# Attention scores from stacked query parts in a two-layer hybrid decoder trunk

## The reference, cut to what matters

```
q  = rope(q)                    # (512, 8, 64), key head kv serves query heads 4*kv + j, j = 0..3
ks, kw = rope(k_sel), rope(k_win)            # (512, 2, 64) each
for br, k, v in ((0, ks, vs), (1, kw, vw)):
    s = einsum('qd,kd->qk', q[:, 4*kv + j], k[:, kv]) * 64 ** -0.5
    p = softmax(where(key <= query, s, -1e30))
    o[br] = p @ v[:, kv]
out = g0 * o_cmp + g1 * o[0] + g2 * o[1]
x = layer_norm(x * alpha + mix(out, scan, pool) @ w_out)
```

## Time and profile before

| | us |
|---|---|
| median of 3 runs | 1748.84 (1747.89 to 1749.04) |
| the profiled execution | 1748.62 |
| its span on the core | 1746.5 |
| TensorE matmuls busy | 1723.6 (99% of the span) |
| VectorE busy | 945.5 (54%) |
| ScalarE busy | 648.7 (37%) |
| GpSimd busy | 115.8 (7%) |
| granted TensorE clock, mean | 0.999 of full speed |

### The profile page before, as it was taken

The page is one execution under the profiler, slowest core; times in us unless marked ns, Lnnn a source line. Parts: engine busy times, 40 slices in busy tenths (PEclk is TensorE's granted clock), DMA queues, the critical chain, the costliest instruction groups (busy, mean ns, idle before and its releaser), DMA issues.

```text
span 1746.5 us, 26759 instructions
## 1 busy us (share of the span) xinstructions
PE 1723.6 (99%) x10172; PEld 1404.4 (80%) x10172; DVE 945.5 (54%) x1527; ACT 648.7 (37%) x1151; POOL 115.8 (7%) x241
## 2 busy tenths in 40 slices
PE   7999999999999999999999999999999999999998
PEld 6788777788888888888888877777888888888886
DVE  5888777554364444422359877864453644444224
ACT  4334666422242222221343346654222422222113
POOL 5600000000000000000045000000000000000000
PEclk9999999999999999999999999999999999999999
DMA  8443111122422222222374431112233222222222
GB/s 270 151 119 89 55 50 48 61 97 99 168 85 84 96 96 97 96 96 97 109 234 122 106 90 56 43 50 72 93 116 118 85 96 96 96 96 96 97 97 85
DMA packets 67134, 174.88 MB, mean 100 GB/s; under 512 B 14448, under 2 KB 25744, under 8 KB 66784
## 3 DMA queue, kind: packets, MB, share of 16 engines
q1 hardware_dynamic: 42560, 151.01, 25.1%
q10 hardware_dynamic: 21888, 13.64, 3.3%
q0 software_dynamic: 2592, 8.92, 1.7%
HBM read 162.27 MB, written 7.08 MB: 97 GB/s over the span
## 4 chain that ended last, share of the span: by engine, by line
PE 91%; DVE 4%; DVEq 2%; ACT 1%; DMA 1%; issue 1%; SPq 0%; ACTq 0%
PE ps L541 20%; PE ps L543 20%; PE ps L542 20%; PE ps L583 5%; PE ps L584 5%; PE ps L582 5%; PE ps L899 2%; PE ps L886 2%; PE ps L872 2%; PE ps L715 1%; PE ps L573 1%; PE ps L562 1%; DMA raw<-wstream 1%; PE ps L564 1%; PE ps L563 1%
## 5 line engine op out<-in xcount | busy, mean ns | idle before, releaser
L541 PE MATMUL ps<-xh,whi 128*128 128x512 f32 x1312 | 519.6, 396 | 2.5 <-ACT gates L1277 2.5
L543 PE MATMUL ps<-xh,wlo 128*128 128x512 f32 x1312 | 511.4, 390 | 0.0
L542 PE MATMUL ps<-xl,whi 128*128 128x512 f32 x1312 | 510.9, 389 | 0.0
L1465 DVE TENSOR_TENSOR wlo<-raw,whi 128x1024 fp32r<-128x1024 f32 x254 | 312.0, 1229 | 324.0 <-ACT whi L1019 318.0
L1019 ACT ACTIVATE whi<-raw 128x1024 fp32r<-128x1024 f32 x248 | 262.0, 1056 | 331.7 <-PE ps L584 216.7
L541 PEld LDWEIGHTS ps<-xh,whi 128*128 128x128 f32 x1312 | 246.4, 188 | 53.0 <-issue 3.6
L543 PEld LDWEIGHTS ps<-xh,wlo 128*128 128x128 f32 x1312 | 246.2, 188 | 52.5
L542 PEld LDWEIGHTS ps<-xl,whi 128*128 128x128 f32 x1312 | 246.6, 188 | 49.0 <-issue 0.5
L582 PE MATMUL ps<-whi,hh 128*128 128x512 f32 x336 | 131.3, 391 | 0.0
L584 PE MATMUL ps<-whi,hl 128*128 128x512 f32 x336 | 130.8, 389 | 0.0
L583 PE MATMUL ps<-wlo,hh 128*128 128x512 f32 x336 | 130.7, 389 | 0.0
(11 more groups left out here) (367 smaller groups left out, 2380.1 us busy)
## 6 DMA issues: line engine op xcount, KB each, us to landing
raw<-wstream SPq DMA_DIRECT2D x264, 512.0 KB, 3.2
w<-w1s SPq DMA_DIRECT2D x16, 512.0 KB, 7.2
sm<-smalls POOLq DMA_DIRECT2D x2, 1060.0 KB, 7.0
xt<-xin ACTq DMA_DIRECT2D x4, 512.0 KB, 6.4
scratch_u<-pa ACTq DMA_DIRECT2D x8, 256.0 KB
toep<-scratch_k ACTq DMA_DIRECT2D x4, 512.0 KB
toep_b<-scratch_k ACTq DMA_DIRECT2D x4, 512.0 KB
xt<-xin POOLq DMA_DIRECT2D x4, 512.0 KB, 4.2
```

Source lines behind the costliest of these rows:

```text
L541: pe.matmul(ps[:, bank, :], wh, hi[:, k, :], start=first and i == 0, stop=False)
L542: pe.matmul(ps[:, bank, :], wh, lo[:, k, :], start=False, stop=False)
L543: m = pe.matmul(ps[:, bank, :], wl, hi[:, k, :], start=False, stop=last and i == len(blocks) - 1)
L1465: dve.tensor_tensor(wlo[:, c % 2, :], raw[:, c % 2, :], whi[:, c % 2, :].bitcast(f32), SUB).then_inc(lo_ready, 1)
```

## The change

It has four parts.

1. `scores` makes four matmuls over all 128 rows, two for each key head. Its stationary operand for key head v (`q_parts[j][v]`) has the high part of that head's queries on one half of the partitions and their low part on the other; its moving operands are `k_high[v]` and `k_low[v]`, the head's keys on both halves. So high by high and low by high come out of one product, and high by low together with low by low, which was left out before, out of the other. The mask is added as before.
2. For this GpSimd copies keys to the other half by three DMAs of 256 KB (`kro_b`, and `kro` itself), after waits on the rotated keys, on the compressed keys and on the first output matrices of the scan. `key_parts` makes two casts and two subtractions of 128 x 1024 in place of one each, and signals `keys_split`. `query_parts` becomes `query_high` (one addition as before, and two casts of 64 x 512) and `query_low` (two subtractions of 64 x 512 with output on the other half). In the loop `query_low` is at u = 5, `gelu_low` goes from u = 5 to 6. Buffers are moved for it; `prob` has two slots in place of three.
3. In the loop, `pool_means` goes from j = 2, u = 4 to 7 to j = 2, u = 6 and 7, and j = 3, u = 3 and 4. ScalarE does the gate output of the first slab of j = 3 ahead of the wait on `gelu_arg`.
4. At the layer norms `turn_back` of the first half comes after three of the six products of the first remaining slab; ScalarE and VectorE do the four groups of the first half ahead of the split of the second slab of the next stage; `first_pair` waits for the first slab, and for the second only ahead of its own quarters.

```diff
     at = big_at + 12288
-    prob = more("prob", [P, 3, 2, S])
+    prob = more("prob", [P, 2, 2, S])
     probt = more("probt", [P, 2, 2, S])
+    kh_b = place("kh_b", at, [P, 2, S], f32r)
+    at += 2 * S
...
+    q_parts = ((q_a0, q_b0), (q_a1, q_b1[0]), (q_a0, q_b0), (q_a1, q_b1[1]))
+    kh_a = place("kh_a", used["sm"][0] + SM["bre"][0], [P, 2, S], f32r)
+    kl_a = place("kl_a", used["kro"][0], [P, 2, S], f32r)
+    kl_b = place("kl_b", used["sm"][0] + SM["wg"][0], [P, 2, S], f32r)
+    kro_b = place("kro_b", used["kl_b"][0], [P, 2, S])
+    k_high, k_low = (kh_a, kh_b), (kl_a, kl_b)
...
                 pool.memset(r8m[:, :, 0:1], 0.0).then_inc(eph_ready, 1)
+                wait(krot_done, l * 3 + 3)
+                pool.wait_ge(kc_psum, l + 1)
+                pool.wait_ge(mats_ready[0], l * 2 + 1)
+                for rows in (slice(0, HD), slice(HD, P)):
+                    pool.dma_start(kro_b[rows, :, :], kro[HD:P, :, :]).then_inc(keys_moved, 16)
+                wait(keys_moved, l * 48 + 32)
+                pool.dma_start(kro[HD:P, :, :], kro[0:HD, :, :]).then_inc(keys_moved, 16)
...
-                token_products(ends[0][0], ends[0][1], 1, 3, k, hi, lo, False).then_inc(slab_done, 1)
+                token_products(ends[0][0], ends[0][1], 1, 3, k, hi, lo, False, (0,))
                 turn_back(n, 0, rt)
+                token_products(ends[0][0], ends[0][1], 1, 3, k, hi, lo, False, (1,)).then_inc(slab_done, 1)
...
-                pe.wait_ge(lo_ready, at + 4)
+                pe.wait_ge(lo_ready, at + 3)
                 for g in range(4):
                     x_quarter(at, 0, g, n * 8)
+                pe.wait_ge(lo_ready, at + 4)
...
-                    qh, ql = qhis[i // 8], qlos[i // 8]
-                    for a, b in ((qh, krh), (ql, krh), (qh, krl)):
-                        for kv in range(2):
-                            rows = slice(64 * kv, 64 * kv + 64)
-                            pe.matmul(ps[:, sbank(i) + kv, 0:n], a[rows, P * t:P * t + P], b[rows, br, 0:n],
-                                      start=a is qh and b is krh, stop=False)
+                    for kv in range(2):
+                        q = q_parts[i // 8][kv]
+                        for k in (k_high[kv], k_low[kv]):
+                            pe.matmul(ps[:, sbank(i) + kv, 0:n], q[:, P * t:P * t + P], k[:, br, 0:n], start=k is k_high[kv], stop=False)
...
                 pe.wait_ge(masks_ready, 2)
+                pe.wait_ge(keys_split, l + 1)
                 pe.wait_ge(q_ready, l * 4 + 2)
...
-                split_end_hi(next_slab + 1, 2, next_slab - 4)
                 for g in range(4):
                     gained(n, 0, g, rt, last)
+                split_end_hi(next_slab + 1, 2, next_slab - 4)
                 split_next_hi(next_slab + 2, next_slab - 2)
...
                         if j < 3:
                             query_out(j + 1, n, 6)
+                        else:
+                            gate_out(13, n, 6)
                         act.wait_ge(gelu_arg, l * 5 + j + 2)
...
-                    if j == 3 and u in (1, 3, 5):
+                    if j == 3 and u in (3, 5):
                         gate_out(13 + u // 2, n, 6)
...
-                split_end_lo(next_slab + 1, 2)
                 second_stats(n, 2, next_slab + 2)
-                for g in range(3):
+                for g in range(4):
                     halves(n, 0, g, rt, last)
                 second_stats(n, 3, next_slab + 2)
                 variances(1)
-                halves(n, 0, 3, rt, last)
+                split_end_lo(next_slab + 1, 2)
                 scalars(n, 1)
...
                     dve.drain()
-                    dve.tensor_copy(krh[:, :, :], kro[:, :, :])
-                    dve.drain()
-                    tt(krl[:, :, :], kro[:, :, :], krh[:, :, :].bitcast(f32), SUB)
+                    dve.wait_ge(keys_moved, l * 48 + 48)
+                    whole = (kro, kro_b)
+                    for v in range(2):
+                        dve.tensor_copy(k_high[v][:, :, :], whole[v][:, :, :])
+                    dve.drain()
+                    for v in range(2):
+                        x = tt(k_low[v][:, :, :], whole[v][:, :, :], k_high[v][:, :, :].bitcast(f32), SUB)
+                    x.then_inc(keys_split, 1)
...
-                def query_parts(j):
+                def query_high(j):
                     q, q_shift, _ = att_bufs(j)
                     dve.drain()
                     tt(q[:, :], qt1[:, :], q_shift[:, :], ADD)
                     dve.drain()
-                    dve.tensor_copy(qhis[j][:, :], q[:, :])
-                    dve.drain()
-                    tt(qlos[j][:, :], q[:, :], qhis[j][:, :].bitcast(f32), SUB).then_inc(q_ready, 1)
+                    for v in range(2):
+                        rows = slice(HD * v, HD * v + HD)
+                        dve.tensor_copy(q_parts[j][v][rows, :], q[rows, :])
+
+                def query_low(j):
+                    q = att_bufs(j)[0]
+                    dve.drain()
+                    for v in range(2):
+                        rows, other = slice(HD * v, HD * v + HD), slice(HD - HD * v, P - HD * v)
+                        x = tt(q_parts[j][v][other, :], q[rows, :], q_parts[j][v][rows, :].bitcast(f32), SUB)
+                    x.then_inc(q_ready, 1)
...
                 rope(0)
-                query_parts(0)
+                query_high(0)
+                query_low(0)
                 scan(l * 4 + 3, 3)
...
+                    if u == 5 and j < 3:
+                        query_low(j + 1)
                     if k0 == 0 and at < 3:
                         split_lo(hl_, first_slab(j) + at + 1)
...
                     if u == 4 and j < 3:
-                        query_parts(j + 1)
-                    if u == 5:
+                        query_high(j + 1)
+                    if u == 6:
                         gelu_low(j)
...
-                    if j == 2 and u > 3:
-                        x = pool_means(u - 4)
-                        if u == 7:
+                    if j == 2 and u > 5:
+                        pool_means(u - 6)
+                    if j == 3 and u in (3, 4):
+                        x = pool_means(u - 1)
+                        if u == 4:
                             x.then_inc(pool_ready, 1)
```

More of the change, by code:

```diff
@@ L141, in build_program @@
     toep = own("toep", [P, 8, P])
-    sm = own("sm", [P, NSM])
     nrm = own("nrm", [P, L, 32])
@@ L151, in build_program @@
     dmaskb = own("dmaskb", [P, P], mybir.dt.bfloat16)
+    sm = own("sm", [P, NSM])
     pa = place("pa", big_at + 8192, [P, 10, S])
@@ L169, in build_program @@
     st = more("st", [P, 16, GP])
+    at = big_at + 17408
     u8_c = more("u8_c", [P, 8, NCH])
@@ L227, in build_program @@
     qraws = (qraw_a, qraw_b)
[L228 to L234, removed]
+    q_a0 = place("q_a0", big_at + 19200, [P, S], f32r)
+    q_b0 = place("q_b0", big_at + 19712, [P, S], f32r)
+    q_a1 = place("q_a1", used["nsh"][0] + 3 * S, [P, S], f32r)
+    q_b1 = [place("q_b1_%d" % n, used["nsl"][0] + n * S, [P, S], f32r) for n in (2, 3)]
+    q_parts = ((q_a0, q_b0), (q_a1, q_b1[0]), (q_a0, q_b0), (q_a1, q_b1[1]))
[4 more added lines that the diff above has]
+    k_high, k_low = (kh_a, kh_b), (kl_a, kl_b)
     qt1 = place("qt1", used["toep"][0] + S, [P, S])
@@ L574, in residual, with token_products @@
                                   start=m == 0, stop=False, is_transpose=True)
-            def token_products(high, low, fh, t, k0, hi, lo, last):
+            def token_products(high, low, fh, t, k0, hi, lo, last, parts=(0, 1)):
                 dst = ps[:, tile_bank(fh, t), :]
-                for q in range(2):
+                for q in parts:
                     a, b = hi[:, k0 + q, P * t:P * t + P], lo[:, k0 + q, P * t:P * t + P]
@@ L885, in turned @@
                             bank, at = turned_at(i, kv)
-                            m = pe.transpose(ps[:, bank, at + P * k:at + P * k + P], prob[:, i % 3, kv, P * k:P * k + P], ident)
+                            m = pe.transpose(ps[:, bank, at + P * k:at + P * k + P], prob[:, i % 2, kv, P * k:P * k + P], ident)
                     m.then_inc(s_tpsum, 1)
@@ L1341, in exps @@
                     for kv in range(2):
-                        x = act.activation(prob[:, i % 3, kv, 0:n], ps[:, sbank(i) + kv, 0:n], ACT.Exp,
+                        x = act.activation(prob[:, i % 2, kv, 0:n], ps[:, sbank(i) + kv, 0:n], ACT.Exp,
                                            bias=tiny[:, 28 + 8 * (i % 3) + kv:29 + 8 * (i % 3) + kv],
@@ L1349, in scale @@
                     act.wait_ge(s_ratio, l * 32 + (i + 1))
-                    act.activation(prob[:, i % 3, 0, 0:n], prob[:, i % 3, 0, 0:n], ACT.Copy, scale=tiny[:, 52 + 2 * (i % 3):53 + 2 * (i % 3)])\
+                    act.activation(prob[:, i % 2, 0, 0:n], prob[:, i % 2, 0, 0:n], ACT.Copy, scale=tiny[:, 52 + 2 * (i % 3):53 + 2 * (i % 3)])\
                        .then_inc(p_first, 1)
@@ L1930, in scale @@
```

(2 more changed lines are left out.)

5 lines of the change are left out of this document (3 added, 2 removed).

## The result

| | before | changed |
|---|---|---|
| median | 1748.93 (1747.89 to 1750.36, 7 runs) | 1755.56 (1754.89 to 1757.49, 7 runs) |
| the profiled execution | 1748.62 | 1757.19 |
| its span | 1746.5 | 1755.0 |
| granted clock, mean | 0.999 | 0.994 |

The ratio is 1.0039 [1.0029, 1.0049]: the changed kernel is 6.6 us slower. Forecast were 1742.0 and a range of 1737.5 to 1747.5, with 0.09 for slower. The prediction was wrong, in direction too.

What follows compares the result with a forecast made beforehand. It took TensorE, with matmuls running 99% of the span, as the bound. Terms of -6.8 + 3.8 - 1.1 - 2.5 + 0 = -6.6 us against the profiled 1748.62 gave 1742.0, range 1737.5 to 1747.5.

Steps and rivals of the forecast that it cites:

- Keys on GpSimd: Three key DMAs before the attention: GpSimd idles from 75.7 us, they are needed by 150.87, so they cost nothing.
- the other terms: All but the key copies: scores -6.8, prologue +3.8, loop -1.1, gate output -2.5, layer norms 0; sum -6.6 us.
- The two on the slower side: Scores: the entrance gap stays, 1752.3 us, chance 0.08; both gaps stay and side-by-side pairs count, 1758.4 us, chance 0.05.
- the larger gain: Rival at layer norms and scores: norms win their 2.1 us and scores 0.15 each, 1737.7 us; chance 0.12.
- the gain at 128 keys: Scores of 128 keys, last transpose to mask: 0.68 us before, 0.57 after, gain given as 0.12.
- Scores: Attention scores on TensorE: four full products replace three half-array pairs, mean gain 0.11 us over 60 scores, -6.8 us.
- Both gaps: Scores, entering and leaving the three half-array pairs: extra time of about 0.19 + 0.09 us, saved by full products.
- Prologue: Attention's start: added VectorE casts and subtractions for keys and queries delay TensorE 1.9 us a layer, +3.8 us.
- Loop: Attention loop: VectorE work moved between units removes TensorE's wait for copied probabilities, -1.1 us.
- Gate output and norms: Gate output ahead of the tanh's wait removes TensorE waits, -2.5 us; at layer norms the wait only moves, 0.

Runs made afterwards that it cites:

- before_with_copies: Kernel before plus only the waits and three key copies, at the changed kernel's place, into a buffer nobody reads: 1763.71 us, 1.0082.
- keys_after_toep: Changed kernel with GpSimd's first key copies waiting until the scan's first matrix, `toep`, has landed: 1746.66 us, 0.9983 of the kernel before.
- no_copies: Changed kernel without the three key copies, both key heads' operands made from `kro` as it stands: 1744.13 us, 0.9972 of the kernel before.
- keys_after_toep_b: Changed kernel with GpSimd's key copies waiting until the scan's next matrix, `toep_in[1]`, has landed: 1746.06 us, 0.9983 of the kernel before.
- gate_and_norms_only: Kernel before with only the gate output moved ahead of the tanh and the change's fourth part, the layer norms: 1746.57 us, 0.9982.
- no_copies_pairs: Changed kernel without the key copies and with scores again as three pairs of half-array products: 1751.49 us, 1.0011 of the kernel before.
- the new order of the prologue: `keys_after_toep_b` with both maxima ahead of the compressed scores and score 0 scaled before the slab split: 1739.67 us, 0.9946 of the kernel before.
- third_copy_late: Changed kernel with the first two key copies at their place, only the third behind the landing of `toep`: 1753.70 us, 1.0023.

## Why the prediction was wrong

**The step that failed** is "Keys on GpSimd": "Cost nothing; if the copies came 60 us late they would go straight onto the chain above". It asked one question of the three DMAs, whether they would be through before `key_parts` needs them, and they were: the last was issued at 99.99 us with a due time near 150. It did not ask what else the 16 DMA engines were doing at 92 us. The last of the copies' waits to end, for the compressed keys (L845, [16.40 <-PE ps L845] in the timeline), let them go at 92.60 us, just as ScalarE starts the scan's round trip, and that had no room: its products came directly at the end of the work ahead of them. `before_with_copies` shows the cost without the rest of the change, `keys_after_toep` shows the rest without the cost. By medians:

| | us |
|---|---|
| forecast | 1742.0 |
| the other terms, short by (`no_copies`, 1744.13) | +2.1 |
| copies, even late (`keys_after_toep_b`, 1746.06) | +1.9 |
| copies at the place of the change (1755.56) | +9.5 |

Against the kernel before, timed beside it (1749.10), `no_copies` gains 5.0 us of the 6.6 forecast, so the second row is 1.6 us by that count. The third row is within the noise, as said above.

The last row is not the waits alone. In the profiled executions the changed kernel reaches the query's products of layer 1 7.65 us later than `keys_after_toep_b` (161.78 and 154.13). TensorE stands for 6.03 us, and the work behind, up to the next slab, takes 6.40 us in place of 4.56, so 1.84 us more at the lower clock (less 0.23 us by which `keys_after_toep_b` comes to these products later). In the second layer it is 4.04 us, and 6.20 in place of 4.14. By these two executions the copies cost more than the 9.5 us of the medians: the changed kernel's was 1.6 us above its median, that of `keys_after_toep_b` 1.4 below.

**No rival had it.** The two on the slower side both made the gain on the scores the uncertain part, and that was the part that held. A transfer that brings a wait of its own was never priced. The chances have a slip besides: the forecast and the larger gain add up to 0.74 and not 0.72, and so faster to 0.78, and the gain at 128 keys is 0.68 - 0.57 = 0.11 and not 0.12. Neither moves the sum.

**Scores: right.** By the last transpose and the mask: 1.04, 0.82, 0.59 and 0.51 us for 512, 384, 256 and 128 keys, forecast 1.02, 0.81, 0.59 and 0.57. Both gaps were a matter of the half arrays. The exchange of the products alone gave 7.4 us (6.1 to 6.7 at an equal clock), forecast 6.8; the 128-key scores gave 0.06 each more than forecast, those of 384 and 512 keys 0.01 and 0.02 less. Of the Trainium skill's advice to split a contraction of 64 into two row tiles ("TensorEngine Tiling (Array Packing)", Performance Considerations) these runs show the limit: with three pairs between full-array work, the pairs lose.

**Prologue: right in size at its place, short in its price.** 2.07 us a layer for 1.9, half-height instructions at the price of full-height ones (0.42 us for a cast of 64 x 512, 0.68 and 0.69 for a subtraction). The waits at the first transposes went from 0.51 to 2.35. That the clock can fall behind such a wait was in none of the terms; it is the likely home of most of the 2.1 us by which `no_copies` misses the forecast: the new order of the prologue gave back 2 us more than the waits it removed, and the executions of `no_copies` at a clock of 0.999 miss the forecast by 0.7 to 1.2 us only. That the clock is lower just there is shown by single traces and not run by run.

**Loop: right.** No wait of TensorE for copied probabilities is left, and none new in the loop. The trace of `gate_and_norms_only` still has that wait, 1.0 us in two, and `no_copies` has not, nor has `no_copies_pairs` with the scores as pairs. So it is not the scores but the rest of the change in the loop that removes it; its parts were not tried one by one.

**Gate output and norms: right.** 2.7 us for 2.5 + 0.

**Open.** Whether late copies cost anything, and why they would. In `keys_after_toep_b` TensorE once pauses 1.2 us in the middle of a run of 32 small products in the second layer, from about 992.9 to 994.1 us, while the copies go (the third is issued at 993.3), and no releaser is named. `gate_and_norms_only`, which has no copies, has such a pause too (0.6 us, at the scan's products of L757), so it is not proof. Also open is why the copies cost the kernel before 14.4 us and the changed one 11.4 (1755.56 less 1744.13). And that the copies delay the round trip by sharing the DMA engines fits the landings, but no run sends them by another way: what is shown is that it depends on when they go.

## What to carry to other kernels

A transfer that is early enough for its own reader need not be free: look up what shares the DMA engines in the window in which it will run, above all round trips through HBM whose result TensorE needs at once, and order it behind them. In this TensorE-bound kernel waits of 4.0 and 6.0 us cost 1.8 to 2.1 us each beyond their length, since the work behind them starts at the lower clock. And when a chain gets longer by a known amount, reordering its queue is worth trying in the same step: here it gave 6.4 us.

## What the runs showed of the hardware that was not expected

- Three copies of 256 KB between partitions, issued beside a 64 KB store and a 512 KB load in packets of some 420 bytes, stretched the store's landing from 3.5 to 5.8 us and the load from at most 9.4 to 12.8.
- With 6 us of idle TensorE (105.35 to 111.38) the granted clock fell to 0.50 and stayed there for up to 5.6 us of work. Behind waits of 2.35 us it was lower (0.91 as a mean of 20 us) in some executions and 1.00 in others. Behind a wait of 2.8 us in the first layer it was 0.50 in the one trace of `third_copy_late`, where the 32 products by `toep` took 1.98 us, and 1.00 in that of `before_with_copies`, where they took 1.15.
- Four full-array products beat three pairs of half-array products, 7.4 us over 64 scores of 128 to 512 columns (0.12 us each; at 512 columns 1.04 us in place of 1.08), though the pairs run fully side by side.
- The wait list of one execution can mislead on size: `before_with_copies` shows 7.5 us of waits for `toep` and a profiled time 5.7 us under its own median. The mean granted clock of each execution, 0.998 there and 0.995 in the others, tells them apart.
